# Query and key norms: one reciprocal-root function of ScalarE and a Newton step on VectorE in place of square root and reciprocal, with another order of the first query tiles

## The chip, the cores and the metric

The kernel runs on one core of a Trainium2 chip. The metric is the device time of one execution in microseconds (us); a profiled execution also has a span, from its first to its last recorded instruction. PE is TensorE, DVE is VectorE, ACT is ScalarE, POOL is GpSimd, SP is SyncE, which here issues DMAs. L1335 is line 1335 of the kernel before.

## What is computed

One layer of a hybrid decoder trunk runs over a prompt of 1024 positions and 8 single new tokens (1032 columns in all, model width 1024): a recurrence and a dilated-window attention with 24 heads of 64, merged by gates, and then a feed-forward block. The change concerns the norm of queries and keys:

```python
def rmsnorm(x, g):
    xf = x.astype(jnp.float32)
    y = xf * lax.rsqrt(jnp.mean(xf * xf, axis=-1, keepdims=True) + EPS)
    return (y * g.astype(jnp.float32)).astype(x.dtype)
...
xn = rmsnorm(x, norm_mix)
lru_x, lru_g, q, k, v = jnp.split(xn @ w_in, SPLITS, axis=-1)
...
q = rmsnorm(q.reshape(B, T, N_ATT_HEADS, HEAD_DIM), q_gain)
k = rmsnorm(k.reshape(B, T, N_ATT_HEADS, HEAD_DIM), k_gain)
```

Everything is float32. A product of two float32 matrices is made of three matmuls of high and low parts.

## The kernel before

Activations lie with features on the 128 partitions and positions along the row. A list named `stream` (L159) gives the weights in the order of use: v, lru, qk, att0 to att2, and so on. Each entry is a loop over pairs of output tiles of 128 features, one for each slot j = 0, 1. For each tile SP loads 512 KB of weights (L329), POOL splits them into a high and a low part with a cast (L448) and a subtraction (L450), and TensorE makes a unit of 72 matmuls (L472: three column chunks, eight row tiles, three products) into PSUM, `ups`, one half for each slot. POOL's split for the next tile of a slot waits until the unit that reads the slot's weights is done.

The qk stage has 12 pairs, i = 0 to 11: 12 query tiles and 12 key tiles, two heads in each. For the tile (i, j):

- ACT's `evac` (L988) copies the tile from PSUM into `tmp(j)`, squares it into `tmp(2+j)` and copies the squares, rounded, into `sq_parts[0]` (L991, L993, L996). It first waits for `qn_done[j]`, that is, until the tile before it in this slot is normed.
- DVE's `square_low` (L1268) writes the low part of the squares into `sq_parts[1]` (L1270).
- TensorE's `stats` (L553) multiplies both parts by `bones_r`, a matrix of ones for each head, so that every position holds its head's sum of squares: four matmuls of 512 columns (L559) into `aux`. There is one `aux` and one `sq_parts` for both slots, so one tile's statistics follow another's. `stats` waits for `qsl_done[j]` (the low squares) and for `rt_done[1-j]` (`aux` has been read).
- ACT's `root` (L1003) takes the square root of sum/64 + eps from `aux` into `tmp(4+j)` (L1006).
- DVE's `normed_qk` (L1332) makes the reciprocal in place (L1335) and multiplies the tile by its gain and the reciprocal (L1337) into `tmp(6+j)`; ACT's `store` (L999) sends that to HBM.

TensorE puts the statistics of one tile between the second and third chunk of the next (L562), from i = 2 on in a loop; before that the order is written out (L570 to L583). The first attention pair (`pair`, L591) takes the last statistics, `stats(1, 11)`, after its first eight pieces. It then waits for the value load, turns V (L614, into `aux`), and makes the first scores (L625) once DVE has passed the `memset` of L1355, which stands behind the last normed tile.

The order of the queues decides much here: each engine runs its instructions in the order written, and waits in front of an instruction hold all that follows. The recurrence's last tile (`recur(KT-1, True)`, L1329) runs on DVE while TensorE has begun the qk stage; its L1286 is the last reader of `tmp(1)`, and its L1289 raises `lru_done`. SP's loads for the first attention pair stand at L396 to L403: `value_load(0, 0)` writes `tmp(2)` and waits for `qsl_done[0]`, and `bias_load(0, 0)` writes into `sq_parts[0]` and waits for `st_done[1]`.

```python
            evac(0, 0)
            act.wait_ge(lru_done, KT)
            act.dma_start(O["lru_out"], sout[:]).then_inc(out_done, 16)
            act.dma_start(O["state_out"], stc[:]).then_inc(out_done, 16)
            root(0, 0)
            evac(0, 1)
            with act.Fori(1, 12) as i:
                root(i - 1, 1)
                evac(i, 0)
                store(i - 1, 0)
                root(i, 0)
                evac(i, 1)
                store(i - 1, 1)
```

Of the kernel before, what the change touches and what calls it, by code (L numbers as in the profile page):

```python
# [23 lines left out]
ALU = mybir.AluOpType  # L24
ACT = mybir.ActivationFunctionType
# [3 lines left out]
P = 128  # L29
D = 1024  # L30
SEQ = 1024
# [4 lines left out]
KT = D // P  # L36
HD = 64
# [7 lines left out]
EPS = 1e-6  # L45
# [47 lines left out]
def build(nc, A, O):  # L93

    with ExitStack() as ctx:
# [3 lines left out]
        def sem(name):  # L99
            return ctx.enter_context(nc.semaphore(name))  # L100
# [7 lines left out]
        big1 = sb("big1", [P, 2, KT, NT], F32R)  # L108
# [14 lines left out]
        bones = sb("bones", [P, P])  # L123
        bones_r = sb("bones_r", [P, P], F32R)
        gq2 = sb("gq2", [P, 2])
        gqk = sb("gqk", [P, 12])
# [7 lines left out]
        epst = sb("epst", [P, 1])  # L134
# [9 lines left out]
        def tmp(n):  # L144

            return x1[:, n, :]

        ups = ctx.enter_context(nc.psum_tensor("ups", [P, 2, NCH, 512], F32))
        aux = ctx.enter_context(nc.psum_tensor("aux", [P, 2, 512], F32))
# [24 lines left out]
        T0, t = {}, 0  # L174
# [5 lines left out]
        def two(name):  # L180

            return [sem(f"{name}{j}") for j in range(2)]
# [21 lines left out]
        conv_done, u_done, z_done = sem("conv_done"), sem("u_done"), sem("z_done")  # L204
        gate_mm, gate_ev, ath_done, m2_done, sqrt_done = sem("gate_mm"), sem("gate_ev"), sem("ath_done"), sem("m2_done"), sem("sqrt_done")
        out_done, lru_done = sem("out_done"), sem("lru_done")

        qsq_done, st_done, rt_done, qn_done = two("qsq_done"), two("st_done"), two("rt_done"), two("qn_done")
        qsh_done, qsl_done = two("qsh_done"), two("qsl_done")
        qn_stored = two("qn_stored")  # L210
        sqc_done = sem("sqc_done")
# [31 lines left out]
        sqs, rms, ul8 = flat[:, 0:192], flat[:, 192:384], flat[0:HG, 400:787]  # L243
# [78 lines left out]
        def _(sp):  # L322
            for name, iters, nk, src, f0, f1, step, k0 in stream:
# [67 lines left out]
                if name == "att0":  # L391
                    first = 1
                    weights(0, 0)
                    weights(0, 1)
                    for n in range(4):
                        sp.wait_ge(v_stored[n], 16)  # L396
                    sp.wait_ge(qn_stored[0], 16 * 8)
                    query_loads(0, 0)
                    sp.wait_ge(qsl_done[0], 12)
                    value_load(0, 0)  # L400
                    sp.wait_ge(bt_fill, 16)
                    sp.wait_ge(st_done[1], 13)
                    bias_load(0, 0)  # L403
# [56 lines left out]
        def _(pe):  # L460
            def unit(name, i, slot, src, nk=KT, parts=(0, 1, 2), ready=None, late=0):

                if 0 in parts:
                    pe.wait_ge(w_split[slot], i + (T0[name] + 2))
                    pe.wait_ge(ps_free[slot], i + (T0[name] + 1 - (12 if T0[name] >= T0["ylru"] else 0)))
                for tiles in (range(nk - late), range(nk - late, nk)):
                    for c in parts:
                        for k in tiles:
                            if ready:
                                ready(c, k)  # L470
                            for w, a in ((0, 0), (0, 1), (1, 0)):
                                ins = nc.tensor.matmul(ups[:, slot, c, 0:CH], wsp[:, slot, w, k, :], src[:, a, k, c * CH:(c + 1) * CH],  # L472
                                                       start=(k == 0 and w + a == 0), stop=(k == nk - 1 and w == 1))
                if NCH - 1 in parts:
                    ins.then_inc(unit_done[slot], 1)
# [77 lines left out]
            def stats(j, i):  # L553

                pe.wait_ge(qsl_done[j], i + 1)
                pe.wait_ge(rt_done[1 - j], i + 1)
                for c in range(2):
                    for a in range(2):
                        ins = nc.tensor.matmul(aux[:, c, :], bones_r[:], sq_parts[a][:, c * 512:(c + 1) * 512], start=(a == 0), stop=(a == 1))  # L559
                ins.then_inc(st_done[j], 1)  # L560
# [5 lines left out]
                    unit("qk", i, j, big1, parts=(2,))  # L566

            pe.sem_inc(rt_done[1], 1)
            pe.sem_inc(st_done[1], 1)
            for c in range(2):  # L570
                unit("qk", 0, 0, big1, parts=(c,))
# [4 lines left out]
            unit("qk", 1, 0, big1, parts=(0,))  # L576
            stats(0, 0)
            unit("qk", 1, 0, big1, parts=(1, 2))
            unit("qk", 1, 1, big1, parts=(0,))
            stats(1, 0)  # L580
            unit("qk", 1, 1, big1, parts=(1,))
            stats(0, 1)
            unit("qk", 1, 1, big1, parts=(2,))  # L583
            with pe.Fori(2, 12) as i:
# [5 lines left out]
            for g in range(NG):  # L590
                def pair(i, first, marks):  # L591
# [14 lines left out]
                    if first:  # L606
                        stats(1, 11)
                        pieces(8, marks[0])
                        pe.wait_ge(ps_free[1], T0["att0"] + 1)
                        pe.wait_ge(rt_done[1], 13)  # L610
                    pe.wait_ge(v_ld, i * 16 + 16 * (4 * g + 1))
                    pe.wait_ge(pt_ev, i * 4 + (16 * g + 1))
                    for b in range(8):
# [3 lines left out]
                    for n in range(6):  # L617
                        if n < 4:
                            pe.wait_ge(sa_done, i * 4 + (16 * g + n + 1))
                            for m in range(2):  # L620
                                b = 2 * n + m
# [17 lines left out]
                        if n >= 2:  # L639
# [3 lines left out]
                            for m in range(2):  # L643
                                b = 2 * q + m
                                nk = nkeys(g, b)
                                for hh in range(2):
                                    at = (2 * m + hh) * (HD + 1)
                                    for k in range(nk):
                                        c = 256 * m + 256 - P * (nk - k)
# [178 lines left out]
        def _(act):  # L828
            step = Chain(act, s_act)
# [158 lines left out]
            def evac(i, j):  # L988
                act.wait_ge(unit_done[j], i + (T0["qk"] + 2))
                act.wait_ge(qn_done[j], i + 1)  # L990
                nc.scalar.activation(chunks(tmp(j)), ups_v[j], ACT.Copy).then_inc(ps_free[j], 1)  # L991
                act.wait_ge(ps_free[j], i + (T0["qk"] + 2))
                nc.scalar.activation(tmp(2 + j)[:, 0:SEQ], tmp(j)[:, 0:SEQ], ACT.Square).then_inc(qsq_done[j], 1)  # L993
                act.wait_ge(qsq_done[j], i + 1)
                act.wait_ge(st_done[1 - j], i + 1)
                nc.scalar.activation(sq_parts[0], tmp(2 + j)[:, 0:SEQ], ACT.Copy).then_inc(qsh_done[j], 1)  # L996
                nc.scalar.activation(sqkv[:, ds(i * 2 + j, 1), :], tmp(j)[:, SEQ:NT], ACT.Copy).then_inc(sqc_done, 1)
# [5 lines left out]
            def root(i, j):  # L1003
                act.wait_ge(st_done[j], i + (1 + j))
                act.wait_ge(qn_done[j], i + 1)
                nc.scalar.activation(tmp(4 + j)[:, 0:SEQ], aux[:].rearrange("p b n -> p (b n)"), ACT.Sqrt, scale=1.0 / HD, bias=epst[:])\  # L1006
                    .then_inc(rt_done[j], 1)

            act.wait_ge(u_done, KT + 1)
            evac(0, 0)  # L1010
            act.wait_ge(lru_done, KT)
            act.dma_start(O["lru_out"], sout[:]).then_inc(out_done, 16)
            act.dma_start(O["state_out"], stc[:]).then_inc(out_done, 16)
            root(0, 0)
            evac(0, 1)
            with act.Fori(1, 12) as i:
                root(i - 1, 1)
                evac(i, 0)
# [177 lines left out]
        def _(dve):  # L1196
            step = Chain(dve, s_dve)
# [70 lines left out]
            def square_low(i, j):  # L1268
                dve.wait_ge(qsh_done[j], i + 1)
                nc.vector.tensor_tensor(sq_parts[1], tmp(2 + j)[:, 0:SEQ], sq_parts[0].bitcast(F32), ALU.subtract).then_inc(qsl_done[j], 1)  # L1270
# [37 lines left out]
            normed(7)  # L1308
            normed_low(6)
            normed_low(7)  # L1310
            nc.vector.tensor_copy(bones_r[:], bones[:])
            for c in range(2):
                nc.vector.tensor_copy(gqk[:, 6 * c:6 * c + 6], gq2[:, c:c + 1].broadcast_to([P, 6]))
            step.step(nc.vector.tensor_scalar(bmrg[:], bmrg[:], 0.5, None, ALU.mult))
            dve.wait_ge(unit_done[1], T0["lru"] + 2)
            nc.vector.tensor_tensor(chunks(GE), ups_v[1], chunks(rinv), ALU.mult).then_inc(ps_free[1], 1)
# [13 lines left out]


            def normed_qk(i, j):  # L1332
                rms_t = tmp(4 + j)[:, 0:SEQ]
                dve.wait_ge(rt_done[j], i + (1 + j))
                step.step(nc.vector.reciprocal(rms_t, rms_t))  # L1335
                dve.wait_ge(qn_stored[j], i * 16 + 16)
                nc.vector.scalar_tensor_tensor(tmp(6 + j)[:, 0:SEQ], tmp(j)[:, 0:SEQ], gqk[:, ds(i, 1)],  # L1337
                                               rms_t, ALU.mult, ALU.mult).then_inc(qn_done[j], 1)

            with dve.Fori(0, 11) as i:  # L1340
                step.loop(i, 2)
                normed_qk(i, 0)
                square_low(i, 1)
                normed_qk(i, 1)
                square_low(i + 1, 0)
            step.end(11)
            step.loop(11, 2, 11)
            normed_qk(11, 0)
            square_low(11, 1)
            normed_qk(11, 1)  # L1350
# [40 lines left out]
            def s_norm():  # L1391
                dve.wait_ge(sqc_done, 36)
                own_qk = sqkv[:, 0:24, :].rearrange("p f b -> p (f b)")
                nc.vector.tensor_tensor(sqs, own_qk, own_qk, ALU.mult).then_inc(sm_dve, 1)
                dve.wait_ge(sm_act, 1)
                step.step(nc.vector.reciprocal(rms, rms))
                for c in range(2):
                    own = sqkv[:, 12 * c:12 * c + 12, :].rearrange("p f b -> p (f b)")
                    step.step(nc.vector.scalar_tensor_tensor(own, own, gqk[:, 6 * c:6 * c + 1], rms[:, 96 * c:96 * c + 96], ALU.mult, ALU.mult))
                dve.sem_inc(sq_normed, 1)  # L1400

            def s_build():
# [161 lines left out]
            for k in range(KT):  # L1564
                j = k % 2
# [105 lines left out]
```

## Time and profile before

| | |
|---|---|
| median of 3 runs | 2072.11 us (2071.22 to 2073.34) |
| the profiled execution | 2071.17 us, its span 2069.4 us |
| mean granted TensorE clock | 0.993 of full speed |
| TensorE busy with matmuls | 2014.0 us (97% of the span) |
| VectorE busy | 905.9 us (44%) |
| ScalarE busy | 509.3 us (25%) |
| GpSimd busy | 552.1 us (27%) |
| HBM traffic | 92 GB/s over the span |

The profile names an engine's busy time, its idle time before an instruction, and what ended that idle time (the releaser, inferred from semaphores). A line of the timeline gives the start, the length, the engine, the line and operation, the tiles (out<-in) and the number of instructions merged; in brackets stands the idle time before it. The granted clock of a window is 1.00 at full speed (2.4 GHz) and 0.50 at half (1.2 GHz). The qk stage runs from about 286 to 587 us of the span.

### The profile page before, as it was taken

Reading aid. Unit: us, or ns where it says so; the run is one execution under the profiler, and the core shown is the slowest. Engines: PE = TensorE matmul, PEld = TensorE weight load, DVE = VectorE, ACT = ScalarE, POOL = GpSimd, SP = SyncE. Lnnn points to the kernel's source line nnn. Section 1 sums busy time; section 2 is a strip of 40 time slices with the busy share of each in tenths; the row PEclk is TensorE's granted clock in tenths of the full one; section 3 lists DMA queues with packets and bytes.
Section 4 is the critical chain, followed back from the end, with each engine's and each line's share of the span. In section 5 each row is a group of like instructions: output and inputs, shape, how many; then the busy total and the mean of one; then the engine's idle time right before and its main releaser. Section 6 shows DMA issues by size and latency. Waiting matters only on the chain.

```text
span 2069.4 us, 32282 instructions
## 1 busy us (share of the span) xinstructions
PE 2014.0 (97%) x12884; PEld 1952.3 (94%) x12884; DVE 905.9 (44%) x919; ACT 509.3 (25%) x726; POOL 552.1 (27%) x325
## 2 busy tenths in 40 slices
PE   7999998999989999999989899999999999999999
PEld 7999997999979999999978899999999999999999
DVE  6666677777762332222266553433311233212331
ACT  5366653333333433333311111201000000000000
POOL 2323332222211111111122143323323232323322
PEclk9999999999999999999999999999999999999999
DMA  5211111222223323334286361111111111111112
GB/s 200 97 44 43 43 46 61 93 90 81 101 97 135 116 97 136 114 111 149 87 307 236 125 239 51 44 48 51 41 51 41 51 42 49 51 41 51 41 59 84
DMA packets 71595, 188.45 MB, mean 91 GB/s; under 512 B 9313, under 2 KB 28796, under 8 KB 70780
## 3 DMA queue, kind: packets, MB, share of 16 engines
q1 hardware_dynamic: 41456, 136.97, 19.5%
q10 hardware_dynamic: 30092, 50.81, 6.7%
q8 instruction: 34, 0.56, 0.1%
q14 instruction: 13, 0.11, 0.0%
HBM read 145.09 MB, written 45.81 MB: 92 GB/s over the span
## 4 chain that ended last, share of the span: by engine, by line
PE 89%; DVE 6%; ACT 1%; issue 1%; DMA 1%; POOL 0%; ACTq 0%; SPq 0%; DVEq 0%; POOLq 0%
PE ups L472 64%; PE ups L600 13%; PE ups L625 3%; PE ups L650 3%; PE aux L637 2%; DVE x L1335 1%; PE aux L538 1%; PE aux L559 1%; PE ups L486 1%; PE aux L614 0%; DVE x L1489 0%; DVE x L1259 0%; DMA x<-o_s 0%; DVE x L1280 0%; ACT x L1076 0%
## 5 line engine op out<-in xcount | busy, mean ns | idle before, releaser
L472 PE MATMUL ups<-big,wsp 128*128 128x344 f32 x9216 | 1477.3, 321 | 9.1 <-POOL wsp L450 6.6
L472 PEld LDWEIGHTS ups<-big,wsp 128*128 128x128 f32 x9216 | 1459.4, 189 | 24.0 <-issue 16.9
L448 POOL CAST wsp<-wraw 128x1024 fp32r<-128x1024 f32 (+2 forms) x160 | 167.8, 1049 | 1485.0 <-issue 724.0
L450 POOL TENSOR_TENSOR wsp<-wraw,wsp 128x1024 fp32r<-128x1024 f32 (+2 forms) x160 | 384.0, 2400 | 12.8
L600 PE MATMUL ups<-big,wsp 128*128 128x344 f32 x1728 | 291.8, 324 | 0.0
L600 PEld LDWEIGHTS ups<-big,wsp 128*128 128x128 f32 x1728 | 272.7, 189 | 5.3 <-issue 5.2
L1335 DVE RECIPROCAL x<-x 128x1024 f32<-128x1024 f32 x24 | 157.3, 6553 | 74.4 <-ACT x L1006 74.4
L1372 DVE SCALAR_TENSOR_TENSOR x<-ups,ext 128x256 f32<-128x256 f32 (+1 forms) x96 | 48.0, 542 | 235.4 <-PE aux L637 147.4
L1181 ACT ACTIVATE ext<-ext 128x1032 f32<-128x1032 f32 x22 | 23.6, 1071 | 482.5 <-DVE ext L1589 482.4
L1591 DVE TENSOR_TENSOR ext<-ups,ext 128x1032 f32<-128x1032 f32 x22 | 27.1, 1233 | 215.4 <-PE ups L472 215.4
L1605 DVE TENSOR_TENSOR x<-ups,x 128x1032 f32 x24 | 29.6, 1233 | 203.6 <-PE ups L472 203.6
L1076 ACT ACTIVATE x<-x,ext 128x128 f32<-128x128 f32 (+1 forms) x192 | 71.2, 442 | 58.8 <-DVE ext L1380 58.4
L1594 DVE TENSOR_TENSOR ext<-ext 128x1032 f32<-128x1032 f32 x22 | 71.3, 3241 | 4.8 <-DVE ext L1591 4.8
L1589 DVE TENSOR_TENSOR ext<-ups,ext 128x1032 f32<-128x1032 f32 x22 | 27.1, 1234 | 105.3 <-PE ups L472 104.9
L625 PE MATMUL ups<-ext 64*128 64x128 f32 (+1 forms) x384 | 67.1, 476 | 4.7 <-DVEq L1357 4.7
L650 PE MATMUL ups<-x 128*128 128x65 f32 x560 | 67.8, 270 | 0.0
L650 PEld LDWEIGHTS ups<-x 128*128 128x128 f32 x560 | 66.8, 192 | 0.0
L1006 ACT ACTIVATE x<-aux,epst 128x1024 f32<-128x1024 f32 x24 | 26.8, 1117 | 132.5 <-PE aux L559 122.9
L625 PEld LDWEIGHTS ups<-ext 64*128 64x128 f32 x384 | 43.5, 281 | 14.6 <-issue 13.1
L1385 DVE COPY x<-ups 128x260 f32<-128x260 f32 x48 | 20.4, 425 | 81.4 <-PE ups L650 81.4
L1066 ACT ACTIVATE x<-aux 128x768 f32<-128x768 f32 (+1 forms) x32 | 28.6, 895 | 83.6 <-PE ups L650 67.5
L1378 DVE TENSOR_REDUCE x<-x 128x2 f32<-128x256 f32 (+1 forms) x96 | 47.6, 538 | 1.6
(190 smaller groups left out, 1147.9 us busy)
## 6 DMA issues: line engine op xcount, KB each, us to landing
wraw<-w_in SPq DMA_DIRECT2D x52, 512.0 KB, 3.4
wraw<-w_ffn_in SPq DMA_DIRECT2D x44, 512.0 KB, 3.2
out_qkv<-x ACTq DMA_DIRECT2D x28, 512.0 KB, 2.7
ext<-out_qkv SPq DMA_DIRECT2D x24, 512.0 KB, 4.3
x<-x_T SPq DMA_DIRECT2D x16, 516.0 KB, 8.2
x<-gate_s SPq DMA_DIRECT2D x16, 516.0 KB, 4.1
wraw<-w_merge SPq DMA_DIRECT2D x16, 512.0 KB, 4.9
wraw<-w_ffn_out SPq DMA_DIRECT2D x16, 512.0 KB, 3.5
```

The source lines that it names most:

```text
L448: nc.gpsimd.tensor_copy(hi, raw).then_inc(w_hi, 1)
L450: nc.gpsimd.tensor_tensor(lo, raw, hi.bitcast(F32), ALU.subtract).then_inc(w_split[slot], 1)
L472: ins = nc.tensor.matmul(ups[:, slot, c, 0:CH], wsp[:, slot, w, k, :], src[:, a, k, c * CH:(c + 1) * CH], start=(k == 0 and w + a == 0), s ...
L600: ins = nc.tensor.matmul(ups[:, 0, c, 0:CH], wsp[:, slot, w, k, :], big1[:, a2, k, c * CH:(c + 1) * CH], start=(k == 0 and w + a2 == 0), s ...
L625: ins = nc.tensor.matmul(s_bank[:, hh, 256 * m + 256 - P * nk:256 * m + 256], toks(QT, g, b)[hr], toks(KTT, g, b, nk)[hr], start=True, sto ...
L637: ins = nc.tensor.transpose(pt_bank[:, hh, c:c + P], SB[:, hh, c:c + P], ident[:])
L650: ins = nc.tensor.matmul(o_bank[:, at:at + HD + 1], PTS[:, hh, c:c + P], VTOK[:, b + 1 - nk + k, hh, :], start=(k == 0), stop=(k == nk - 1))
L1076: ins = nc.scalar.activation(SB[:, hh, cols], SB[:, hh, cols], ACT.Exp, bias=NM[:, 2 * m + hh:2 * m + hh + 1])
L1335: step.step(nc.vector.reciprocal(rms_t, rms_t))
L1372: ins = nc.vector.scalar_tensor_tensor(SB[:, :, cols], s_bank[:, :, cols], SCALE, BT[:, :, 0:P * nk][:, :, ::-1], ALU.mult, ALU.add)
L1378: ins = nc.vector.tensor_reduce(OT[:, 2 * n + m, :, HD + 1], SB[:, :, cols], AX_X, ALU.max)
L1594: step.step(nc.vector.tensor_tensor(ext[:, 1, 0:NT], ext[:, 0, 0:NT], ext[:, 1, 0:NT], ALU.mult))
```

## The change

ScalarE's `root` becomes one function, the reciprocal root of the absolute value, with eps as its bias. The division by 64 moves into `bones_r`. VectorE's reciprocal gives way to one Newton step of products: with s the mean of squares in `aux` and y the function's value, t = (s + eps) y, then t = t y, then t = (t - 3) y, and the tile is multiplied by its gain times -0.5 and by t. The first product reads `aux`, so `aux` is free only after it; a new semaphore, `nt_done`, says so and takes the place of `rt_done` in TensorE's waits. The products use `tmp(2+j)`, where the squares were, so SP's first value load (into `tmp(2)`) waits for the last normed query tile (`qn_done[0]`). The gains of the new tokens' norms are read from `gq2`, since `gqk` now holds the factor -0.5.

Among the first tiles, ACT evacuates the tile (0, 1) before the root of (0, 0), behind a wait for the last reader of `tmp(1)`, and issues the two output DMAs after that root. VectorE makes the low squares of each tile ahead of the norm of the tile before it. TensorE takes the statistics of (0, 1) before the unit of (1, 1) instead of after its first chunk.

```diff
@@ SP, loads of the first attention pair
-                    sp.wait_ge(qsl_done[0], 12)
+                    sp.wait_ge(qn_done[0], 13)
                     value_load(0, 0)
@@ TensorE
             def stats(j, i):
                 pe.wait_ge(qsl_done[j], i + 1)
-                pe.wait_ge(rt_done[1 - j], i + 1)
+                pe.wait_ge(nt_done[1 - j], i + 1)
...
             stats(0, 0)
             unit("qk", 1, 0, big1, parts=(1, 2))
-            unit("qk", 1, 1, big1, parts=(0,))
             stats(1, 0)
-            unit("qk", 1, 1, big1, parts=(1,))
+            unit("qk", 1, 1, big1, parts=(0, 1))
             stats(0, 1)
             unit("qk", 1, 1, big1, parts=(2,))
...
                         pe.wait_ge(ps_free[1], T0["att0"] + 1)
-                        pe.wait_ge(rt_done[1], 13)
+                        pe.wait_ge(nt_done[1], 13)
@@ ScalarE
-                nc.scalar.activation(tmp(4 + j)[:, 0:SEQ], aux[:].rearrange("p b n -> p (b n)"), ACT.Sqrt, scale=1.0 / HD, bias=epst[:])\
+                nc.scalar.activation(tmp(4 + j)[:, 0:SEQ], aux[:].rearrange("p b n -> p (b n)"), ACT.Abs_reciprocal_sqrt, bias=epst[:])\
                     .then_inc(rt_done[j], 1)
             act.wait_ge(u_done, KT + 1)
             evac(0, 0)
+            act.wait_ge(z_done, KT + 1)
+            evac(0, 1)
             act.wait_ge(lru_done, KT)
+            root(0, 0)
             act.dma_start(O["lru_out"], sout[:]).then_inc(out_done, 16)
             act.dma_start(O["state_out"], stc[:]).then_inc(out_done, 16)
-            root(0, 0)
-            evac(0, 1)
@@ VectorE
-            nc.vector.tensor_copy(bones_r[:], bones[:])
+            nc.vector.tensor_scalar(bones_r[:], bones[:], 1.0 / HD, None, ALU.mult)
             for c in range(2):
-                nc.vector.tensor_copy(gqk[:, 6 * c:6 * c + 6], gq2[:, c:c + 1].broadcast_to([P, 6]))
+                nc.vector.tensor_scalar(gqk[:, 6 * c:6 * c + 6], gq2[:, c:c + 1].broadcast_to([P, 6]), -0.5, None, ALU.mult)
...
             def normed_qk(i, j):
-                rms_t = tmp(4 + j)[:, 0:SEQ]
+                y, t = tmp(4 + j)[:, 0:SEQ], tmp(2 + j)[:, 0:SEQ]
                 dve.wait_ge(rt_done[j], i + (1 + j))
-                step.step(nc.vector.reciprocal(rms_t, rms_t))
+                step.step(nc.vector.scalar_tensor_tensor(t, aux[:].rearrange("p b n -> p (b n)"), EPS, y, ALU.add, ALU.mult))
+                dve.sem_inc(nt_done[j], 1)
+                step.step(nc.vector.tensor_tensor(t, t, y, ALU.mult))
+                step.step(nc.vector.scalar_tensor_tensor(t, t, -3.0, y, ALU.add, ALU.mult))
                 dve.wait_ge(qn_stored[j], i * 16 + 16)
                 nc.vector.scalar_tensor_tensor(tmp(6 + j)[:, 0:SEQ], tmp(j)[:, 0:SEQ], gqk[:, ds(i, 1)],
-                                               rms_t, ALU.mult, ALU.mult).then_inc(qn_done[j], 1)
+                                               t, ALU.mult, ALU.mult).then_inc(qn_done[j], 1)
-            with dve.Fori(0, 11) as i:
-                step.loop(i, 2)
+            square_low(0, 1)
+            normed_qk(0, 0)
+            square_low(1, 0)
+            normed_qk(0, 1)
+            with dve.Fori(1, 11) as i:
+                step.loop(i, 6, 1)
                 normed_qk(i, 0)
                 square_low(i, 1)
                 normed_qk(i, 1)
                 square_low(i + 1, 0)
```

## Rows read from the trace of the kernel before

**Rows 1.** The page's busy table: busy us, share of the span, instructions.

```profile
PE 2014.0 (97%) x12884; PEld 1952.3 (94%) x12884; DVE 905.9 (44%) x919; ACT 509.3 (25%) x726; POOL 552.1 (27%) x325
```

**Rows 2.** TensorE's waits, 275 to 640 us: releaser, us in total, times, longest.

```profile
PE aux L559 <- DVE ext_r L1270: 12.2, 3, 6.5
PE ups L625 <- DVEq L1357: 4.7, 1, 4.7
```

**Rows 3.** The timeline of the first query tiles.

```profile
298.69 2.07 DVE L1286 TENSOR_TENSOR x<-x 128x1032 f32<-128x1032 f32 x1
...
302.04 11.49 PE L472 MATMUL ups<-big,wsp 128*128 128x344 f32 x72
303.59 1.23 DVE L1289 TENSOR_TENSOR big<-x,big 128x1032 fp32r<-128x1032 f32 x1
...
306.12 1.12 ACT L1006 ACTIVATE x<-aux,epst 128x1024 f32<-128x1024 f32 x1 [9.60 <-issue]
...
309.93 1.04 POOL L448 CAST wsp<-wraw 128x1024 fp32r<-128x1024 f32 x1 [6.92 <-PE ups L472]
...
316.54 1.20 PE L559 MATMUL aux<-ext_r,bones_r 128*128 128x512 f32 x4 [3.01 <-DVE ext_r L1270]
...
327.98 2.07 PE L559 MATMUL aux<-ext_r,bones_r 128*128 128x512 f32 x4 [6.48 <-DVE ext_r L1270]
...
329.86 12.70 PE L472 MATMUL ups<-big,wsp 128*128 128x344 f32 x72
```

**Rows 4.** The timeline of one steady half step.

```profile
563.08 1.09 PE L559 MATMUL aux<-ext_r,bones_r 128*128 128x512 f32 x4
...
565.36 6.55 DVE L1335 RECIPROCAL x<-x 128x1024 f32<-128x1024 f32 x1 [3.06 <-ACT x L1006]
...
568.12 1.04 POOL L448 CAST wsp<-wraw 128x1024 fp32r<-128x1024 f32 x1 [8.74 <-PE ups L472]
...
569.24 2.41 POOL L450 TENSOR_TENSOR wsp<-wraw,wsp 128x1024 fp32r<-128x1024 f32 x1
570.15 1.06 ACT L996 ACTIVATE ext_r<-x 128x1024 fp32r<-128x1024 f32 x1
...
571.95 1.29 DVE L1337 SCALAR_TENSOR_TENSOR x<-x,gqk 128x1024 f32<-128x1024 f32 x1
573.15 1.22 DVE L1270 TENSOR_TENSOR ext_r<-x,ext_r 128x1024 fp32r<-128x1024 f32 x1
...
575.34 1.09 PE L559 MATMUL aux<-ext_r,bones_r 128*128 128x512 f32 x4
```

**Rows 5.** The timeline from the last key tile to the first scores.

```profile
580.37 1.04 POOL L448 CAST wsp<-wraw 128x1024 fp32r<-128x1024 f32 x1 [8.72 <-issue]
...
597.23 1.66 PE L625 MATMUL ups<-ext 64*128 64x128 f32 x8 [4.71 <-DVEq L1357]
597.57 1.28 ACT L1058 ACT_TABLE_LOAD   x1 [8.54 <-DVE x L1337]
...
598.82 5.54 PE L600 MATMUL ups<-big,wsp 128*128 128x344 f32 x24
```

**Rows 6.** Windows of 2 us: busy us of each engine, PEclk, DMA share, GB/s.

```profile
316.00:318.00 2.00, 1.46 (x7) 1.28 (x8) 0.48 (x1) 0.23 (x1) 0.00 (x0) 1.00 0.18 72
...
326.00:328.00 2.00, 0.02 (x1) 0.02 (x1) 1.93 (x2) 0.00 (x0) 0.00 (x0) 0.50 0.00 0
```

**Rows 7.** DVE beside POOL: two timeline rows, L1280's lengths (ns), L1605.

```profile
142.05 3.47 POOL L450 TENSOR_TENSOR wsp<-wraw,wsp 128x1024 fp32r<-128x1024 f32 x1
143.30 4.37 DVE L1280 TENSOR_TENSOR_SCAN x<-x 128x1024 f32<-128x1024 f32 x1
...
L1280 DVE TENSOR_TENSOR_SCAN x<-x x8: 2291/4362/4370, 119.4 to 294.7; 128x1024 f32<-128x1024 f32 x8
...
1509.61 1.23 DVE L1605 TENSOR_TENSOR x<-ups,x 128x1032 f32 x1 [4.50 <-PE ups L472]
```

**Rows 8.** The page's DMA issues: KB each, median us to landing.

```profile
x<-out_qkv SPq DMA_DIRECT2D x12, 512.0 KB, 4.7
```

More of the change, by code:

```diff
@@ L208, in build @@
         qsq_done, st_done, rt_done, qn_done = two("qsq_done"), two("st_done"), two("rt_done"), two("qn_done")
+        nt_done = two("nt_done")
         qsh_done, qsl_done = two("qsh_done"), two("qsl_done")
@@ L568, in _ @@
             pe.sem_inc(rt_done[1], 1)
+            pe.sem_inc(nt_done[1], 1)
             pe.sem_inc(st_done[1], 1)
@@ L1345, in _ @@
                 square_low(i + 1, 0)
-            step.end(11)
-            step.loop(11, 2, 11)
+            step.end(10)
+            step.loop(11, 6, 11)
             normed_qk(11, 0)
@@ L1398, in s_norm @@
                     own = sqkv[:, 12 * c:12 * c + 12, :].rearrange("p f b -> p (f b)")
-                    step.step(nc.vector.scalar_tensor_tensor(own, own, gqk[:, 6 * c:6 * c + 1], rms[:, 96 * c:96 * c + 96], ALU.mult, ALU.mult))
+                    step.step(nc.vector.scalar_tensor_tensor(own, own, gq2[:, c:c + 1], rms[:, 96 * c:96 * c + 96], ALU.mult, ALU.mult))
                 dve.sem_inc(sq_normed, 1)
```

## Prediction

> **What bounds the kernel now.** I read the page's busy table first: TensorE has a matmul under way in 2014.0 of 2069.4 us [rows 1]. Other engines matter only where they make it wait, so the table of TensorE's waits is read next, cut to the stage that the diff touches. It has two lines [rows 2]: the head-sum matmuls of the norms (L559) waited 12.2 us in three places for DVE's L1270, and the first scores (L625) waited 4.7 us in one place. The third view, the timeline, places them. Two are among the first query tiles, 3.01 us at 316.54 and 6.48 us at 327.98 [rows 3]; the third is what is left of 12.2, 2.7 us, before the last head sums, at 586.7 (the L1270 of 573.15 [rows 4] one period of 12.26 us later, and its 1.22); the fourth stands at 597.23 [rows 5]. Sum: 16.9 us. The windows add the clock: after the 3.01 us gap TensorE still had 1.00 (2.4 GHz), after the 6.48 us gap 0.50 (1.2 GHz) [rows 6]. In the rows this shows as 2.07 us for four head-sum matmuls that take 1.09 in steady state, and 12.70 us for 72 matmuls that take 11.49 [rows 3, 4], 2.2 us together. Between 342 and 576 us TensorE waits for nothing: one half step, head sums to head sums, is 575.34 - 563.08 = 12.26 us [rows 4], and DVE's 6.55 us reciprocal lies beside matmuls. So this change can give at most 16.9 us of gaps and some 4 us of slow clock, and it can lose in the 22 half steps if its new chain outgrows 12.26 us.
>
> **The first tiles.** If TensorE never waited, it would save 3.01 + 6.48 + (2.07 - 1.09) + (12.70 - 11.49) = 11.7 us here. Now the new order, from the same rows. L1286 ends at 300.76 [rows 3] and frees the tile for evac(0,1): three ACT operations of about 1.05 us (L996 is one [rows 4]), so its high squares are there at 304.0. L1289 ends at 304.82 and releases both square_low(0,1), 1.22 us [rows 4], to 306.05, and root(0,0). The new function needs its table: one load of 1.28 us [rows 5], which takes the place of the two DMA issues that stood before the root (304.82 to 306.12 [rows 3]); the moved issues then lie in ACT's wait for the next head sums. I take the new function at the old root's 1.12 us: root ends at 307.3. DVE's first product reads PSUM; nearest row L1605, 1.23 us [rows 7]: 308.6, and nt_done frees aux. TensorE has run 48 of the 72 matmuls by 302.04 + 7.66 = 309.7, so stats(1,0) waits for nothing: the 3.01 us go.
>
> Then comes POOL. Its cast for the next weights asks at 309.93 [rows 3], just when DVE's second product ends (309.8). Where both wanted to run [rows 7], POOL's subtraction asked at 142.05, under a DVE product of two SBUF tiles, and took 3.47 us where it takes 2.41 in steady state [rows 4]; DVE's next operation, at 143.30, took 4.37 where its shortest is 2.29. They ran in turn, and the one that waited went first. The old reciprocal, 6.55 us beside cast and subtraction of full length [rows 4], met none of this; three of the four new operations and square_low have two SBUF operands.
>
> The Trainium skill says the same as a rule, and against this change: SBUF — State Buffer, section "Who interferes with whom", has a DVE instruction with two SBUF inputs contend with a GpSimd instruction that reads SBUF, for its whole length. The trace agrees (the 3.47 and 4.37 us); by that page the sum is the one with the lock below, without it the first rival's.
>
> With the lock the first normed tile is done at 313.3 (third product first) or 315.8 (cast first, then POOL's 2.41 us in front of the last product). Then evac(1,0) 3.2, square_low(1,0) 1.22, first product 1.23: nt_done[1] at 319.0 or 321.5. TensorE, after stats(1,0) and 48 matmuls, is at stats(0,1) at 318.3: a new wait of 0.7 to 3.2 us. If the table is loaded before L1289 ends, all is 1.2 us earlier and the wait is gone. I take 2.0: **gain 9.7**, bounds 8.5 and 11.7. A gap of 3.01 us left the clock at 1.00 [rows 6], so I count no fall.
>
> **The steady half steps.** DVE starts at 565.36 [rows 4]. First product to 566.6, second (1.22, as L1270) to 567.85, third (1.29, as L1337) to 569.2. POOL asked at 568.12, so cast to 570.2, last product to 571.5, subtraction to 573.9, square_low to 575.1; the head sums start at 575.34. Where an operation had waited its remainder was about 0.14 us shorter than its length alone (143.30 + 4.37 less 142.05 + 3.47 is 2.15, against 2.29 [rows 7]), which puts square_low nearer 574.6. Before it was 573.15 + 1.22 = 574.4. Slack 0.2 to 0.7 us: **cost 0**, but little is left, and every 0.1 us over the period costs 22 x 0.1 = 2.2 us. POOL ends 2 us later, against a next use of that weight slot one period on. The wait for nt_done instead of rt_done lets go some 9 us before the next head sums.
>
> **The end of the stage.** normed_qk(11,0) starts one period after 565.36 [rows 4], at 577.6. With POOL's cast asking at 580.37 [rows 5] the same sum gives square_low at 586.8 to 587.0: the wait that ended at 586.7 stays. Without the lock it ends at 584.8, 1.9 us sooner. After it POOL is idle, and the chain to the first scores is root, normed_qk(11,1), memset: 6.55 + 1.29 become 1.23 + 1.22 + 1.29 + 1.29 + 0.1 of handoffs = 5.1, so L625 starts at 594.5 instead of 597.23: 2.7 us. The gap ahead of it is then 2.0 us instead of 4.71, shorter than the 3.01 us after which the clock stayed [rows 6]: the 24 matmuls of 5.54 us [rows 5] come back to 11.49/3 = 3.8, the eight scores of 1.66 to about 1.1: 2.2 us. **Gain 4.9**, bounds 2.7 (clock falls all the same) and 6.8.
>
> SP's value load now waits for qn_done[0] (583.6) instead of qsl_done; it lands about 4.7 us after issue [rows 8], 588.3, and TensorE turns V only after the head sums and 24 more matmuls, 587.0 + 0.95 + 3.83 = 591.8: hidden by 3.5 us, beyond that each us costs one. Queued behind it on SP is only the bias load, which waits for the last head sums in any case. The scaled copies (L1311, L1313) and s_norm's other gain column keep their number and sizes: nothing.
>
> **Sum.** The execution of the profile took 2071.17 us (span 2069.4 and 1.8 around). 2071.17 - 9.7 - 4.9 = 2056.6; the median of the three runs is 0.94 above the profiled one, so **2057.5**. What follows is bound by TensorE, so a shift carries to the end.
>
> **The rivals.** (a) POOL never gets between the products, or late enough to cost nothing: 11.7 + 6.8 = 18.5, 2053.6. For it: at 309.93 the order hangs on 0.1 us, and the last product may still slip in front of POOL. Against: the turns that the two engines took in the stage before [rows 7]. 15%.
> (b) The order of the first tiles doesn't do what it is said to: square_low(1,0) still stands behind normed_qk(0,0) and evac(1,0), the wait at stats(0,1) is 3.2 us, and the clock falls at both ends. 11.7 - 3.2 - 2.2 = 6.3, and 2.7: 9.0, 2063. For it: the 315.8 branch. Against: gaps of 2.7 and 3.01 us passed without a fall. 11%.
> (c) Slower: the loop head sums, root, four DVE operations, square_low outgrows the period. Its place is the 22 half steps, its price 22 times the excess; it eats the gain from 14.6/22 = 0.66 us of excess, and from 0.85 on the kernel is slower by over 0.2%. A table load before every root (1.28) and 0.24 us for each of three waits with a loop count would make the loop 11.6 + 2.0 = 13.6: 22 x 1.34 - 14.6 = 15 slower, 2087. For it: the slack is down to 0.2 to 0.7. Against: the old root sat in the same loop with Copy and Square, and no load stands between 563.08 and 575.34. 5%.
> (d) The same, by 0.5 us of excess from handoffs: 11 of 14.6 lost, 2069. 7%.
>
> **How the numbers follow.** The forecast has 62%. Its own bounds are 18.5 and 8.5 + 2.7 = 11.2 of gain, 2053.6 to 2061; with (b) the range is 2052.5 to 2064, which leaves out (c), (d) and a little. A change can be told from none at 0.2%, 4.1 us: faster 0.88, same 0.07, slower 0.05.
>
> **What would show it.** Right: no wait at stats(1,0); one of 0.7 to 3.2 us at stats(0,1); clock 1.00 from 310 to 345; a period of 12.26 us with no wait of L559 in it; POOL's cast and subtraction lengthened between DVE's products; last head sums still waited for; L625 some 2.7 us earlier after them. Wrong: a wait in the steady half steps, a table load per half step, or the new root longer than 1.12 us.

## The result, and the profile after

The changed kernel takes 2057.86 us (median of 4, 2056.75 to 2059.27) against 2072.73 us for the kernel before (median of 4, 2071.22 to 2076.70): a ratio of 0.9926, 95% interval 0.9913 to 0.9939, 14.9 us less. The forecast was 2057.5 us.

The page of the kernel after, its span and busy table, beside [rows 1]:

```profile
span 2055.0 us, 32389 instructions
...
PE 2011.3 (98%) x12884; PEld 1949.7 (95%) x12884; DVE 897.4 (44%) x967; ACT 509.8 (25%) x727; POOL 591.4 (29%) x325
```

DVE has 48 instructions more and is busy 8.5 us less; POOL, with not one instruction more, is busy 39 us longer. TensorE's waits of the stage, 275 to 640 us, beside [rows 2] (releaser: us in total, times, longest):

```profile
PE aux L560 <- DVE ext_r L1272: 3.1, 2, 2.8
PE aux L638 <- ACT x L1078: 1.0, 1, 1.0
PE ups L626 <- DVEq L1366: 1.0, 1, 1.0
```

Of 16.9 us of gaps 4.1 are left. The middle line stood in the kernel before too, as a third line of its table, `PE aux L637 <- ACT x L1076: 1.0, 1, 1.0`, which [rows 2] and the prediction leave out; the change didn't touch it. In the changed kernel the head sums are L560, the four operations of `normed_qk` L1337, L1339, L1340 and L1342, `square_low` is L1272, POOL's cast and subtraction are L449 and L451, and the first scores L626.

The timeline of the first tiles, beside [rows 3]:

```profile
304.63 1.28 ACT L1007 ACT_TABLE_LOAD   x1
...
305.93 1.12 ACT L1007 ACTIVATE x<-aux,epst 128x1024 f32<-128x1024 f32 x1
...
309.71 1.22 DVE L1340 SCALAR_TENSOR_TENSOR x<-x 128x1024 f32<-128x1024 f32 x1
...
310.04 1.09 PE L560 MATMUL aux<-ext_r,bones_r 128*128 128x512 f32 x4
310.37 1.46 POOL L449 CAST wsp<-wraw 128x1024 fp32r<-128x1024 f32 x1 [6.90 <-PE ups L473]
...
310.97 1.94 DVE L1342 SCALAR_TENSOR_TENSOR x<-x,gqk 128x1024 f32<-128x1024 f32 x1
...
318.79 0.77 PEld L560 LDWEIGHTS aux<-ext_r,bones_r 128*128 128x128 f32 x4 [0.40 <-issue]
318.82 1.17 PE L560 MATMUL aux<-ext_r,bones_r 128*128 128x512 f32 x4
...
331.60 1.20 PE L560 MATMUL aux<-ext_r,bones_r 128*128 128x512 f32 x4 [0.27 <-DVE ext_r L1272]
```

The head sums at 310.04 and 318.82, which waited 3.01 and 6.48 us, follow the matmuls ahead of them with next to no gap. One steady half step, beside [rows 4]:

```profile
552.38 1.09 PE L560 MATMUL aux<-ext_r,bones_r 128*128 128x512 f32 x4
...
554.66 1.22 DVE L1337 SCALAR_TENSOR_TENSOR x<-aux,x 128x1024 f32<-128x1024 f32 x1 [3.08 <-ACT x L1007]
...
557.29 1.23 DVE L1340 SCALAR_TENSOR_TENSOR x<-x 128x1024 f32<-128x1024 f32 x1
557.42 2.00 POOL L449 CAST wsp<-wraw 128x1024 fp32r<-128x1024 f32 x1 [6.93 <-PE ups L473]
...
558.55 1.94 DVE L1342 SCALAR_TENSOR_TENSOR x<-x,gqk 128x1024 f32<-128x1024 f32 x1
...
559.50 3.26 POOL L451 TENSOR_TENSOR wsp<-wraw,wsp 128x1024 fp32r<-128x1024 f32 x1
...
560.53 3.30 DVE L1272 TENSOR_TENSOR ext_r<-x,ext_r 128x1024 fp32r<-128x1024 f32 x1
...
564.48 0.81 PEld L560 LDWEIGHTS aux<-ext_r,bones_r 128*128 128x128 f32 x4
564.64 1.09 PE L560 MATMUL aux<-ext_r,bones_r 128*128 128x512 f32 x4
```

Five operations take turns: third product, cast, last product, subtraction, low squares. The first keeps its length; the other four are lengthened, each by the one that it found running (2.00 against 1.04 us, 1.94 against 1.29, 3.26 against 2.41, 3.30 against 1.22 in [rows 4]). The two on POOL make 1.8 us in a half step, and so its 39 us. The low squares end at 563.83, and the weights of the head sums are loaded at 564.48: 0.65 us to spare. The end of the stage, beside [rows 5]:

```profile
571.75 3.21 POOL L451 TENSOR_TENSOR wsp<-wraw,wsp 128x1024 fp32r<-128x1024 f32 x1
...
572.80 3.24 DVE L1272 TENSOR_TENSOR ext_r<-x,ext_r 128x1024 fp32r<-128x1024 f32 x1
576.10 1.02 PEld L560 LDWEIGHTS aux<-ext_r,bones_r 128*128 128x128 f32 x4 [3.09 <-DVE ext_r L1272]
576.10 1.74 PE L560 MATMUL aux<-ext_r,bones_r 128*128 128x512 f32 x4 [2.81 <-DVE ext_r L1272]
...
577.64 4.99 PE L601 MATMUL ups<-big,wsp 128*128 128x344 f32 x24
...
584.51 0.93 PE L626 MATMUL ups<-ext 64*128 64x128 f32 x8 [1.01 <-DVEq L1366]
```

and two windows of it, columns as in [rows 6], in which the granted clock fell after the gap of 2.81 us:

```profile
576.00:578.00 2.00, 1.90 (x6) 1.58 (x7) 0.04 (x1) 0.12 (x1) 0.00 (x0) 0.63 0.05 10
578.00:580.00 2.00, 2.00 (x9) 2.00 (x8) 0.97 (x1) 0.99 (x1) 0.00 (x0) 0.52 0.63 171
```

### The profile page after: what moved, and what is told of

It reads as the page before. It is cut to its first block, busy times and chain, and to the rows that moved or that the text cites. A ratio compares the mean times of both kernels' runs of the same rounds, so it can differ in the third digit from the quotient of the medians.

```text
span 2055.0 us, 32389 instructions
## 1 busy us (share of the span) xinstructions
PE 2011.3 (98%) x12884; PEld 1949.7 (95%) x12884; DVE 897.4 (44%) x967; ACT 509.8 (25%) x727; POOL 591.4 (29%) x325
## 4 chain that ended last, share of the span: by engine, by line
PE 88%; DVE 6%; ACT 2%; issue 1%; DMA 1%; POOL 0%; SPq 0%; ACTq 0%; DVEq 0%; POOLq 0%
PE ups L473 64%; PE ups L601 13%; PE ups L626 3%; PE ups L651 3%; PE aux L638 2%; PE aux L539 1%; PE aux L560 1%; PE ups L487 1%; DMA wraw<-w_branch_att 1%; PE aux L615 0%; DVE x L1498 0%; DVE x L1261 0%; DVE ext_r L1272 0%; DVE x L1282 0%; ACT x L1078 0%
## 5 line engine op out<-in xcount | busy, mean ns | idle before, releaser
L449 POOL CAST wsp<-wraw 128x1024 fp32r<-128x1024 f32 (+2 forms) x160 | 191.2, 1195 | 1431.3 <-issue 689.1
L451 POOL TENSOR_TENSOR wsp<-wraw,wsp 128x1024 fp32r<-128x1024 f32 (+2 forms) x160 | 399.9, 2500 | 12.8
L1272 DVE TENSOR_TENSOR ext_r<-x,ext_r 128x1024 fp32r<-128x1024 f32 x24 | 70.7, 2947 | 4.4 <-ACT ext_r L997 3.3
L626 PE MATMUL ups<-ext 64*128 64x128 f32 (+1 forms) x384 | 66.4, 472 | 1.0 <-DVEq L1366 1.0
L1337 DVE SCALAR_TENSOR_TENSOR x<-aux,x 128x1024 f32<-128x1024 f32 x24 | 29.4, 1224 | 64.3 <-ACT x L1007 64.3
L626 PEld LDWEIGHTS ups<-ext 64*128 64x128 f32 x384 | 43.1, 278 | 10.9 <-issue 9.4
```

Source lines behind the costliest of these rows:

```text
L449: nc.gpsimd.tensor_copy(hi, raw).then_inc(w_hi, 1)
L451: nc.gpsimd.tensor_tensor(lo, raw, hi.bitcast(F32), ALU.subtract).then_inc(w_split[slot], 1)
L626: ins = nc.tensor.matmul(s_bank[:, hh, 256 * m + 256 - P * nk:256 * m + 256], toks(QT, g, b)[hr], toks(KTT, g, b, nk)[hr], start=True, sto ...
```

## The experiments

Executions differ by some us before the qk stage begins (last section), so beside each ratio to the kernel before stand two stretches read from the trace of one execution. "First" runs from the first head sums of the stage to those of the third query tile of slot 0, "last" from the last head sums of the steady run to the first transposes of probabilities (L637 before, L638 after). The kernel before has 354.66 - 301.11 = 53.55 and 605.35 - 575.34 = 30.01, the changed kernel 343.96 - 301.56 = 42.40 and 590.40 - 564.64 = 25.76: gains of 11.15 and 4.25 us. In the prediction and in the expectations of e1 and e2, `stats` and the head sums have the slot first, as in the code: the head sums of (1, 0) are those of slot 1, pair 0. For `evac`, `root`, `square_low` and `normed_qk` the pair stands first.

| kernel | ratio to the kernel before, 95% interval | first, us | last, us |
|---|---|---|---|
| before | 1 | 53.55 | 30.01 |
| changed | 0.9926 (0.9913 to 0.9939) | 42.40 | 25.76 |
| e8: changed, again | 0.9925 (0.9912 to 0.9939) | 42.39 | 25.82 |
| e10: changed, a third time | 0.9938 (0.9924 to 0.9951) | 42.42 | 26.76 |
| e1: order alone | 0.9998 (0.9986 to 1.0010) | 51.57 | 29.88 |
| e2: function and products alone | 0.9962 (0.9950 to 0.9974) | 50.67 | 25.24 |
| e7: TensorE's old order | 0.9944 (0.9926 to 0.9962) | 46.36 | 26.77 |
| e3: POOL waits once | 0.9917 (0.9890 to 0.9944) | 42.40 | 24.73 |
| e6: POOL waits, pieces moved | 0.9912 (0.9897 to 0.9926) | 42.38 | 22.13 |
| e9: e6 again | 0.9911 (0.9896 to 0.9926) | 42.41 | 22.12 |
| e4: one product more | 1.0018 (1.0005 to 1.0032) | 48.90 | 30.03 |
| e5: no Newton step (two runs) | 0.9895 (0.9877 to 0.9913) | 41.48 | 21.35 |

**The two parts, each alone.** My theory was that order and shorter chain need each other; the rivals, that one of them does it by itself. First the order, on the kernel before:

```diff
             stats(0, 0)
             unit("qk", 1, 0, big1, parts=(1, 2))
-            unit("qk", 1, 1, big1, parts=(0,))
             stats(1, 0)
-            unit("qk", 1, 1, big1, parts=(1,))
+            unit("qk", 1, 1, big1, parts=(0, 1))
             stats(0, 1)
@@ ScalarE and VectorE: the changed kernel's order, with Sqrt and reciprocal
```

> The new order of the first tiles on all three engines, with the old square root and reciprocal. If the parts need each other: the 3.01 us wait goes, about 1 us is left at the head sums of (0, 1), but two norms of 7.9 us now stand one behind the other on DVE ahead of the low squares of (1, 1), so a new wait of about 4.4 us comes before the head sums of (1, 1); the last gaps (2.7 and 4.7 us) stay as in the kernel before. Gain over the kernel before 4 to 6 us. Rival, the order alone brings what the first tiles gained (11.2 us): gain 11, no wait over 1 us among the first tiles. Rival, the order does nothing without the shorter chain: gain 0.

Three lines of its timeline, DVE, ACT and TensorE:

```profile
326.74 3.28 DVE L1337 SCALAR_TENSOR_TENSOR x<-x,gqk 128x1024 f32<-128x1024 f32 x1
...
330.11 1.03 ACT L990 ACTIVATE x<-ups 128x1032 f32<-128x1032 f32 x1 [7.47 <-DVE x L1337]
...
339.20 2.07 PE L559 MATMUL aux<-ext_r,bones_r 128*128 128x512 f32 x4 [6.38 <-DVE ext_r L1270]
```

The waits at the second and third head sums went (0 and 0.91 us), and a new one of 6.38 came one tile later, with the clock fallen again (2.07 us for the four matmuls). I had put it at 4.4. The other 2 us are the last multiplication of the norm at 326.74, which found POOL's subtraction running and took 3.28 us instead of 1.28; it releases ACT's evacuation, on which the next low squares hang. The first stretch gained 2.0 us; the whole, where I had expected 4 to 6, nothing that can be told from the second rival's 0. Then the function and the products in the old order, an edit that takes the changed kernel's three reordered places back:

```diff
-            stats(1, 0)
-            unit("qk", 1, 1, big1, parts=(0, 1))
+            unit("qk", 1, 1, big1, parts=(0,))
+            stats(1, 0)
+            unit("qk", 1, 1, big1, parts=(1,))
             stats(0, 1)
@@ ScalarE: root(0, 0) and its DMAs ahead of evac(0, 1) again
@@ VectorE: normed_qk(i, 0), square_low(i, 1), ... from i = 0 again
```

> The new function and the products, in the old order of the first tiles. If the parts need each other: the wait at the head sums of (1, 0) stays at 3 us, since POOL's cast and subtraction get between DVE's products there; the one of (0, 1) falls from 6.5 to about 3.9 us; the end is as in the changed kernel (4.3 us sooner). Gain over the kernel before 7 to 9 us, the upper end if the clock doesn't fall at the first tiles. Rival, the shorter chain alone does it and the order is ornament: gain 14 to 15, no wait over 1 us among the first tiles.

```profile
319.23 2.08 PE L560 MATMUL aux<-ext_r,bones_r 128*128 128x512 f32 x4 [4.01 <-DVE ext_r L1272]
...
328.86 1.19 PE L560 MATMUL aux<-ext_r,bones_r 128*128 128x512 f32 x4 [2.38 <-DVE ext_r L1272]
```

The gain is 0.4%, as the theory said: 2.9 us among the first tiles and 4.8 at the end. How the first two waits share it I had wrong (4.0 and 2.4, expected 3 and 3.9): the first root began 6.2 us after the first head sums (309.03 and 302.81) where the changed kernel has 4.4 (305.93 and 301.56), since the table load stood behind the two DMA issues. The clock fell behind the first of these gaps (2.08 us for the head sums). So at the first tiles 2.0 and 2.9 us of the parts alone stand against 11.15 of both; at the end only the shorter chain counts.

**TensorE's order.** The changed kernel with the old three lines on TensorE alone (the first half of the diff above):

> The changed kernel with TensorE's old order alone (the head sums of (0, 1) slot behind the first chunk of the next unit). If TensorE's order is needed to hide ACT's and DVE's work: root(0, 1) and with it evac(1, 0) come 3.9 us later, and a wait of about 3 us appears at the head sums of the second query tile of slot 0; 3 us slower than the changed kernel, gain over the kernel before about 11.5. Rival, only the order on ACT and DVE counts: as the changed kernel, gain 14 to 15.

```profile
320.41 1.23 DVE L1273 TENSOR_TENSOR ext_r<-x,ext_r 128x1024 fp32r<-128x1024 f32 x1 [6.29 <-ACT ext_r L998]
...
322.97 1.17 PE L560 MATMUL aux<-ext_r,bones_r 128*128 128x512 f32 x4 [3.08 <-DVEq L1339]
```

The 3 us wait is there: DVE stood idle for 6.29 us for squares that ACT could only copy after the later root. The first stretch lost 4.0 us, by that wait and a clock of 0.53 and 0.62 in the windows from 324 to 328 us behind it; the rival falls. The 1.0 us of the last stretch isn't shown to be the edit's: the changed kernel's own third execution (e10) has the same 26.76 us there, with the clock fallen at the same place.

**POOL between DVE's products.** At the end of the stage POOL's split for the second weight tile of the attention stage was made to wait until the last low squares are written:

```diff
+                if name == "att0":
+                    first = 1
+                    split(name, nk, 0, 0)
+                    pool.wait_ge(qsl_done[1], 12)
+                    split(name, nk, 0, 1)
                 with pool.Fori(first, iters) as i:
```

> The changed kernel, where POOL's split of the second weight tile of the attention stage waits until the last low squares are written. If POOL's subtraction in front of the last low squares is what holds the last head sums: the low squares take 1.22 instead of 3.24 us, the wait before the last head sums falls from 2.81 to about 0.8 us, the clock stays at 1.00 there, and the second group of scores comes about 2.6 us sooner; 2 to 3.6 us faster than the changed kernel, gain over the kernel before 17 to 18. Rival, ACT's copy of the high squares is what is late: wait and time as in the changed kernel.

```profile
572.63 1.23 DVE L1277 TENSOR_TENSOR ext_r<-x,ext_r 128x1024 fp32r<-128x1024 f32 x1 [0.70 <-ACT ext_r L1002]
573.90 1.20 PE L565 MATMUL aux<-ext_r,bones_r 128*128 128x512 f32 x4 [0.80 <-DVE ext_r L1277]
...
581.77 1.15 PE L631 MATMUL ups<-ext 64*128 64x128 f32 x8 [2.02 <-DVEq L1371]
...
582.85 5.34 PE L606 MATMUL ups<-big,wsp 128*128 128x344 f32 x24
```

The low squares take 1.23 us and the wait falls to 0.80, as expected, so POOL's turn was the cause of 2.0 of its 2.81 us; the rest is ACT's copy (DVE idle 0.70 for L1002). But only 1.0 us of the 2.6 arrived: the gap at the first scores grew to 2.02 us and the clock fell there (24 matmuls in 5.34 us) instead of behind the gap before the head sums. The medians don't tell this kernel from the changed one: the two intervals in the table overlap. So the next kernel also filled that gap. Its edit moves four pieces in all, not five as I wrote ahead of the run: one in front of the last head sums, three more between them and the first scores.

```diff
-        FIRST_PIECES = (16, 24, 32, 38, 42, 46, 48)
+        FIRST_PIECES = (20, 24, 32, 38, 42, 46, 48)
@@ pair, beside the edit on POOL
-                    pieces(0, 8)
+                    pieces(0, 9 if first else 8)
                     if first:
                         stats(1, 11)
-                        pieces(8, marks[0])
+                        pieces(9, marks[0])
```

> The changed kernel with POOL's split waiting for the last low squares, and with five of TensorE's pieces moved from behind the first scores to in front of them (one before the last head sums, four after). If idle TensorE in front of the first scores is what is left, and with it the clock: the 2.02 us wait at the first scores falls under 0.6 us, the clock stays at 1.00 from 572 to 590, and the first transposes of probabilities come about 3.4 us sooner than in the changed kernel; gain over the kernel before 17 to 18.5 us. Rival, the wait only moves behind the first scores (to the exponentials): the same first gap closed, but a new one of 2 us or more there, gain as the changed kernel.

```profile
578.56 1.20 PE L565 MATMUL aux<-ext_r,bones_r 128*128 128x512 f32 x4 [0.32 <-DVE ext_r L1277]
...
586.42 0.93 PE L631 MATMUL ups<-ext 64*128 64x128 f32 x8 [0.61 <-DVEq L1371]
...
591.25 0.87 PE L643 MATMUL aux<-ident,x 128*128 128x128 f32 x6 [0.74 <-ACT x L1083]
```

All gaps from 570 to 606 us are under 0.8 us, every window there shows a clock of 1.00, and the last stretch is 3.6 us shorter than the changed kernel's. The medians, 2056.86 us and 2057.32 for the changed kernel run beside it (e8), didn't show it clear of scatter. So both ran once more (e9 and e10):

> The kernel with POOL's wait and the moved pieces once more, beside the changed kernel of the same call, since the two intervals of the call before overlap: the trace had its first transposes of probabilities 3.7 us sooner after the first head sums, so its median should lie 2 to 4 us under the changed kernel's; rival, later stages give the 3.7 us back and the medians lie within 1 us.

2052.63 us (2050.61 to 2055.97) against 2059.99 (2056.93 to 2061.26). The medians alone leave open how much this version gains (0.5 us the first time, 7.4 the second), since scatter of the program's start is in them. Counted from the first head sums to the end of the span, its two profiled executions took 1749.0 and 1748.6 us, the changed kernel's three 1753.4, 1752.3 and 1755.1: 3.3 to 6.5 us less. The last stretch has 3.6 to 4.6 of it.

**The slack of the steady half step.** One more product of two SBUF tiles in each norm:

```diff
                 step.step(nc.vector.scalar_tensor_tensor(t, t, -3.0, y, ALU.add, ALU.mult))
+                step.step(nc.vector.tensor_tensor(y, t, y, ALU.mult))
```

> The changed kernel with one more product of two SBUF tiles in each norm on DVE (its result is not used). If the slack of the steady half step is the 0.65 us that the trace shows: the low squares end about 0.45 us after TensorE needs them, the head sums wait in every half step, the period goes from 12.26 to about 12.7 us, and the time is 9 to 13 us above that of the changed kernel. Rival, the chain has room because POOL's turns give way: period 12.26, 1 to 3 us slower from the first and last tiles alone.

Its time is 2076.51 us, 19.2 above the changed kernel run beside it (e8), and above the kernel before. One steady half step:

```profile
452.64 1.20 PE L560 MATMUL aux<-ext_r,bones_r 128*128 128x512 f32 x4 [0.23 <-DVE ext_r L1272]
...
461.11 3.10 DVE L1343 SCALAR_TENSOR_TENSOR x<-x,gqk 128x1024 f32<-128x1024 f32 x1 [0.24 <-DVE x L1341]
464.14 1.21 DVE L1272 TENSOR_TENSOR ext_r<-x,ext_r 128x1024 fp32r<-128x1024 f32 x1
465.40 1.20 PE L560 MATMUL aux<-ext_r,bones_r 128*128 128x512 f32 x4 [0.23 <-DVE ext_r L1272]
```

The period is 465.40 - 452.64 = 12.76 us: 0.50 over the old one, and the 18 of them between the two stretches are 8.9 us longer, as expected. Too small were the two ends: 6.5 us in the first stretch and 4.3 in the last, where I had put 1 to 3 together. So the time fell outside the 9 to 13 us expected, and a little more than half of the loss lies at the ends.

**What the Newton step costs.** Without it (the three products taken out, the gains' factor back to 1):

```diff
-                step.step(nc.vector.scalar_tensor_tensor(t, aux[:].rearrange("p b n -> p (b n)"), EPS, y, ALU.add, ALU.mult))
                 dve.sem_inc(nt_done[j], 1)
-                step.step(nc.vector.tensor_tensor(t, t, y, ALU.mult))
-                step.step(nc.vector.scalar_tensor_tensor(t, t, -3.0, y, ALU.add, ALU.mult))
```

> The changed kernel without the Newton step: ScalarE's value goes straight into the last product, so the roots are only as good as the function. If the steady half steps hide the products and the last tiles don't: period 12.26 as before, the last low squares no longer behind POOL's subtraction, no wait at the first scores, 4 to 5 us faster than the changed kernel, all of it at the two ends of the stage. Rival, the products cost nothing anywhere: the time of the changed kernel.

The time is 2051.73 us, 5.6 under the changed kernel run beside it (e8): 0.9 us in the first stretch, 4.4 in the last, nothing in the half steps between (220.68 us in both kernels). No run here shows what accuracy the step buys.

## Why the prediction was right, point by point

**First tiles: right, the gain too small.** 11.15 us against 9.7, inside the bounds of 8.5 and 11.7. I had booked 2.0 us for a wait at the head sums of the second query tile, between 0.7 and 3.2, with 0 if the table came early. It came early: the load at 304.63 ran while ACT still waited for `lru_done`, 0.7 us ahead of the end of the recurrence. With that DVE's third product began at 309.71, before POOL asked at 310.37, which was the better branch. Waits of 0.4 and 0.27 us are what is left (the first is the idle time of the weight load at 318.79).

**Steady half steps: right.** The period is (564.64 - 343.96) / 18 = 12.26 us, cost 0, slack 0.65 where I had 0.2 to 0.7. The order of turns is the one worked out there: third product, cast, last product, subtraction, low squares. e4 shows that the slack was needed: 0.5 us of excess in the period and the gain is gone, together with what the same product costs at the ends. The price of 2.2 us for each 0.1 us was for the period, and it counted 22 periods; 18 lie between the two stretches, and 0.50 us over cost 8.9 there, 1.8 for each 0.1. A wait of 0.23 us in e4's rows lengthened the period by 0.50, so the table of waits alone gives half. Of the other half 0.11 is the head sums' own (1.20 us instead of 1.09); the rest is overlap with the matmuls ahead, which head sums that wait don't have.

**The end: inside its bounds, with one step wrong.** 4.25 us against 4.9, bounds 2.7 and 6.8 (4.19 and 3.25 in e8 and e10). The wait before the last head sums stayed, 2.81 us, and e3 shows it to be POOL's. The step that failed is that a gap shorter than 3.01 us leaves the clock alone: after 2.81 us it fell to half, and the head sums and the next 24 matmuls took 1.74 + 4.99 instead of 1.20 + 3.93, 1.6 us more. What I had as a gap of 2.0 us at the first scores was 1.0 for the same reason (slow matmuls filled it), and there the clock stayed, as forecast. The first scores were to start 2.7 us earlier after the last head sums; they started 2.1 earlier (8.41 against 10.55 us), since the head sums themselves took 0.54 us longer.

**Hidden costs: right.** SP's value load went out at 572.78 and V was turned at 582.46 with no wait for it. The moved DMA issues (305.40 and 305.78) lay beside ACT's own work.

**The sum.** 11.15 + 4.25 = 15.4 us in the two stretches against 14.6 booked; the spans differ by 14.4, since the changed run began its qk stage 0.45 us later and took some 0.6 longer behind it. That the median of the forecast hit within 0.4 us is luck: both terms were off, by 1.4 and by 0.7 the other way.

**Rivals.** (a) was half true: at the first tiles the order fell DVE's way, in the half steps and at the end POOL took its turns. (b) failed at the first tiles and held in its clock at the end. (c) didn't come, but it can: e4 crossed its point with one product. Both its place and its point were too narrow, though. It put the price into the half steps alone and the loss of the whole gain at 0.66 us of excess; 0.50 was enough, since the two ends lost 10.8 us as well. (d) didn't come.

## What to carry to other kernels

- When an operation that leaves POOL alone is replaced by several with two SBUF operands, lay them out in turn with POOL's and count each of POOL's into the chain. Then see which of DVE's results is the one that TensorE waits for, and let POOL wait where it has time: one wait and four moved pieces shortened the last stretch by 3.6 to 4.6 us here.
- Two edits to one chain may each be worth little (2.0 and 2.9 us) and much together (11.15): an edit that removes one wait can uncover the next (6.38 us in e1).
- Read the slack of a hidden loop from the trace before and after. 0.65 us was left of a 12.3 us period, and one product of 1.2 us more turned a gain of 15 us into a loss of 3; over half of that came from the ends of the loop, so price those too.

## What the runs showed of the hardware that was not expected

The clock of TensorE fell or stayed after gaps of the same length. It stayed after 3.01 and 2.69 us in the kernel before; it fell after the same gap of 2.69 us in e1, after 2.81 us in the changed kernel, and after 2.02 us at the scores of e3. In the third execution of the changed kernel (e10), as in e7, it stayed through a gap of 2.82 us and fell after the next one, of 2.02, whose 24 matmuls took 5.59 us. The kernel before, e1 and e10:

```profile
586.68 1.20 PE L559 MATMUL aux<-ext_r,bones_r 128*128 128x512 f32 x4 [2.69 <-DVE ext_r L1270]
587.71 3.93 PE L600 MATMUL ups<-big,wsp 128*128 128x344 f32 x24
```

```profile
585.85 1.49 PE L559 MATMUL aux<-ext_r,bones_r 128*128 128x512 f32 x4 [2.69 <-DVE ext_r L1270]
587.14 5.23 PE L599 MATMUL ups<-big,wsp 128*128 128x344 f32 x24
```

```profile
579.02 1.19 PE L560 MATMUL aux<-ext_r,bones_r 128*128 128x512 f32 x4 [2.82 <-DVE ext_r L1272]
580.05 3.93 PE L601 MATMUL ups<-big,wsp 128*128 128x344 f32 x24
...
586.88 0.93 PE L626 MATMUL ups<-ext 64*128 64x128 f32 x8 [2.02 <-DVEq L1366]
587.73 5.59 PE L601 MATMUL ups<-big,wsp 128*128 128x344 f32 x24
```

What decides between the two was not tried. So a gap of 2 to 3 us must be priced with the fall (about 1.6 us here) as a real possibility.

Executions also differ before this stage. One window of the start (columns as before), first e6, then the changed kernel:

```profile
20.00:40.00 20.00, 20.00 (x96) 17.09 (x95) 12.85 (x23) 10.27 (x12) 0.00 (x0) 0.80 0.04 10
```

```profile
20.00:40.00 20.00, 20.00 (x117) 18.12 (x116) 15.99 (x25) 11.95 (x16) 3.41 (x2) 1.00 0.04 9
```

A lower clock in this window went with a first head-sum time of 306.06 instead of 301.56 us. The two kernels are alike up to there, so 4.5 us of scatter come from the start, as much as many of the edits compared here. The other profiled executions go the same way: the seven of all twelve that show 1.00 from 0 to 40 us have their first head sums at 300.83 to 301.71 us, the five with less at 302.26 to 306.06. What lowers the clock there was not tried.
